# Prompt attention by chunks of 512 keys, and the setup loads in another order

## What is computed

```python
def diff_attend(q, k, v, q_pos, k_pos, lam):
    s = jnp.einsum('ntkgch,nskch->nkgcts', q, k, preferred_element_type=jnp.float32) * SCALE
    mask = k_pos[None, :] <= q_pos[:, None]
    s = jnp.where(mask, s, -jnp.inf)
    p = jax.nn.softmax(s, axis=-1)
    a = p[:, :, :, 0] - lam * p[:, :, :, 1]
    return jnp.einsum('nkgts,nskv->ntkgv', a, v.astype(jnp.float32))
```

## Time and profile before

| | us |
|---|---|
| median of 3 runs | 2490.93 |
| lowest, highest | 2490.03, 2493.18 |
| profiled execution | 2487.62 |
| its span, first to last instruction | 2485.8 |

### The profile page before, as it was taken

The page is one execution under the profiler, slowest core; times in us unless marked ns, Lnnn a source line. Parts: engine busy times, 40 slices in busy tenths (PEclk is TensorE's granted clock), DMA queues, the critical chain, the costliest instruction groups (busy, mean ns, idle before and its releaser), DMA issues. The chain is left out here.

```text
span 2485.8 us, 37618 instructions
## 1 busy us (share of the span) xinstructions
PE 2170.9 (87%) x13193; PEld 1995.5 (80%) x13193; DVE 1155.8 (46%) x1914; ACT 971.2 (39%) x1572; POOL 1279.6 (51%) x682
## 2 busy tenths in 40 slices
PE   4999999999279998999889987877777787898998
PEld 4999999999279998999889985655665666666998
DVE  3698889889845003222100005555555554346101
ACT  4455555555444112111121125555555554234111
POOL 2799999999733324433311125555455552224232
PEclk7999999999669999999989987888888887997999
DMA  6112111121223222223222230000000005882221
GB/s 234 51 54 65 60 60 60 48 63 53 84 60 122 69 94 88 69 77 94 90 82 95 86 128 26 18 26 18 17 26 17 9 1 155 255 262 76 60 77 70
DMA packets 182037, 192.51 MB, mean 77 GB/s; under 512 B 11435, under 2 KB 147060, under 8 KB 181332
## 3 DMA queue, kind: packets, MB, share of 16 engines
q1 hardware_dynamic: 181952, 191.48, 24.4%
HBM read 145.52 MB, written 47.63 MB: 78 GB/s over the span
## 5 line engine op out<-in xcount | busy, mean ns | idle before, releaser
L222 POOL TENSOR_TENSOR w_lo<-w_raw,w_hi 128x1024 fp32r<-128x1024 f32 x116 | 279.6, 2411 | 603.3 <-ACT w_hi L218 603.3
L242 PE MATMUL ps<-Hhi,w_hi 128*128 128x352 f32 x1704 | 560.5, 329 | 18.3 <-POOL w_lo L222 11.7
L242 PE MATMUL ps<-Hhi,w_lo 128*128 128x352 f32 x1704 | 550.9, 323 | 0.0
L242 PE MATMUL ps<-Hlo,w_hi 128*128 128x352 f32 x1704 | 549.9, 323 | 0.0
L777 DVE SCALAR_TENSOR_TENSOR ps<-U,dww,ps 128x512 f32<-128x512 f32 x608 | 403.1, 748 | 0.0
L218 ACT ACTIVATE w_hi<-w_raw 128x1024 fp32r<-128x1024 f32 x116 | 122.1, 1053 | 665.7 <-PE ps L242 244.6
L696 POOL TENSOR_TENSOR pool_acc<-pool_acc,prod 128x1024 f32<-128x1024 f32 x144 | 346.3, 2405 | 31.0 <-ACT prod L645 22.7
L242 PEld LDWEIGHTS ps<-Hhi,w_hi 128*128 128x128 f32 x1704 | 321.9, 189 | 27.9 <-POOL w_lo L222 18.4
L242 PEld LDWEIGHTS ps<-Hlo,w_hi 128*128 128x128 f32 x1704 | 323.1, 190 | 2.1
L242 PEld LDWEIGHTS ps<-Hhi,w_lo 128*128 128x128 f32 x1704 | 322.1, 189 | 0.0
L645 ACT ACTIVATE prod<-U,dww 128x1024 f32<-128x1024 f32 x176 | 197.0, 1147 | 249.8 <-POOL pool_acc L696 143.3
(11 more groups left out here) (237 smaller groups left out, 3876.4 us busy)
## 6 DMA issues: line engine op xcount, KB each, us to landing
w_raw<-conv_w_in SPq DMA_DIRECT2D x48, 512.0 KB, 4.1
w_raw<-attn_w_in SPq DMA_DIRECT2D x40, 512.0 KB, 4.7
kpage<-cache_k SPq DMA_DIRECT2D x64, 256.0 KB, 3.0
vpage<-cache_v SPq DMA_DIRECT2D x64, 256.0 KB
res<-Y SPq DMA_DIRECT2D x2, 4224.0 KB, 21.4
gate<-sg SPq DMA_DIRECT2D x16, 528.0 KB, 4.0
sgl<-gate SPq DMA_DIRECT2D x16, 528.0 KB, 3.7
xres<-res SPq DMA_DIRECT2D x16, 528.0 KB, 3.9
```

The costliest lines, as they stand in the source:

```text
L222: pool.tensor_tensor(wlo[s][:, :, :], raw[s][:, :, :], whi[s][:, :, :].bitcast(F32), ALU.subtract).then_inc(w_lo, 1)
L242: mm = pe.matmul(ps[:, 3 * dst + c, 0:CH], w[:, k, :], r(k)[:, c * CH:(c + 1) * CH], start=start and k == 0 and w is whi[s] and r is rhs_h ...
```

## The change

Attention is written in steps y = 0 .. 47 per group, twelve per head. A tile of up to 512 keys is one step as before; a wider one is two: its first 512 keys, then the rest with the mask. Every step uses one pair of banks, alternating. The second step of a wide tile takes the minimum of the two negated maxima (L1720), and the sums and weights of its first step are corrected by e = exp(new negated maximum - old negated maximum): a distance on DVE (L1723), an exponential on ACT (`weight`, L1647), two operations on DVE for the sums (L1732, L1734), and on POOL two scalings of the first 512 keys, of p1 by T0 x e / sum (`N_U`, L1740 on DVE) and of p0 by e. `stats` has 20 columns per tile and 32 tiles. The squares of the sums are taken once per head. `LAG` is 5 steps. `p0` has eight buffers of the widths needed, `p1` four. `coefficients` stands after `maxes` on DVE. The query's parts for the next head are made at step 1 instead of tile 4, new values at step 9, before `hi`.

In the setup, weights are loaded after the small loads, `stg` and the write of Y after the square roots; x tiles share semaphores in groups; the roots, reciprocals and the spread come before the turning of `dwin`; `stg` lies in another place and is turned in the convolution block, after PE's first unit; its copies stand behind the norm on ACT and DVE, and the wait for the written Y is on ACT and DVE there.

The diff, cut to its core:

```diff
-                for s, kind in ((0, 0), (1, 1)):
-                    sp.dma_start(raw[s][:, :, :], conv_src(0, kind)).then_inc(raw_in[s], 16)
                 for r, name, n in ((C_NG1, "norm_g", 16), ...
...
+                sp.dma_start(dwin[:, :], a["conv_dw_w"][0]).then_inc(dw_in, 16)
                 sp.dma_start(ptab[:, :], a["page_table"].rearrange("(o b) p -> o (b p)", o=1)).then_inc(lam_in, 16)
-                sp.dma_start(stg[:, :, :], st_src).then_inc(st_loaded, 16)
+                for s, kind in ((0, 0), (1, 1)):
+                    sp.dma_start(raw[s][:, :, :], conv_src(0, kind)).then_inc(raw_in[s], 16)
                 sp.wait_ge(xe_act, NXT)
                 sp.wait_ge(xe_dve, NXT)
+                sp.wait_ge(Norm.std_ready, 1)
+                sp.dma_start(stg[:, :, :], st_src).then_inc(st_loaded, 16)
                 sp.dma_start(res_d[0], Y[:, :, :]).then_inc(res_out[0], 16)
-                sp.wait_ge(res_out[0], 16)
...
                         unit_by_tile(pe, n, e, e, norms[0])
+                        if first and s == 0:
+                            turn_state()
                         pe.wait_ge(sg_done, j)
...
+                act.wait_ge(st_dve, JT // 4)
+                act.wait_ge(res_out[0], 16)
...
-        LAG = 2
+        LAG = 5
+        UNITS = 12
+        VALUES = {10: (0, (0,)), 11: (0, (1, 2)), 12: (0, (3,)),
+                  17: (1, (0, 1)), 18: (1, (2, 3)), 19: (1, (4, 5)), 20: (1, (6, 7))}
+        OUTPUTS, TOTALS, SUMS = {13: 0, 21: 1}, {14: 0, 22: 1}, {15: 0, 23: 1}
+        NEW_VALUES, NEXT_Q = 9, 1
...
+        def score_ap(x, n, c):
+            return ps[:, 2 * (unit_of(x, n) % 2) + c, 0:width(x, n)]
...
+                    if u >= 2:
+                        pe.wait_ge(exp_done, 2 * NU * g + 2 * (u - 2) + 2)
...
+                def exp(g, x, n, c):
+                    if n == 0:
+                        act.wait_ge(mx_done, 2 * NU * g + 2 * unit_of(x, n) + c + 1)
+                    else:
+                        act.wait_ge(run_done, 4 * GH * g + wides(x) + 1)
+                    if n == 0 and c == 0 and x >= QT:
+                        act.wait_ge(tg_done, NU * g + tgroups(x - QT)[-1][0] + 1)
+                    if n == 0 and c == 1 and x >= 4:
+                        act.wait_ge(comb_done, NX * g + x - 3)
...
+                def weight(g, x):
+                    act.wait_ge(dist_done, 4 * GH * g + wides(x) + 1)
+                    act.activation(stat(x, N_E, 2), stat(x, N_D, 2), ACT.Exp).then_inc(weight_done, 1)
...
+                        for c in range(2):
+                            exp(g, x, n, c)
+                        if n == 1:
+                            weight(g, x)
...
+                    if 0 <= y - LAG < top:
+                        hi(g, y - LAG)
...
+                    if n == 1:
+                        dve.wait_ge(mx_done, 2 * NU * g + 2 * u + 2)
+                        dve.tensor_tensor(stat(x, N_NM + 2, 2), stat(x, N_NM, 2), stat(x, N_NM + 2, 2), ALU.min
+                                          ).then_inc(run_done, 1)
+                        dve.wait_ge(run_done, 4 * GH * g + wides(x) + 1)
+                        dve.tensor_tensor(stat(x, N_D, 2), stat(x, N_NM + 2, 2), stat(x, N_NM, 2), ALU.subtract
+                                          ).then_inc(dist_done, 1)
...
+                    if wide:
+                        dve.wait_ge(weight_done, 4 * GH * g + wides(x) + 1)
+                        step_up(dve.tensor_tensor(stat(x, N_ES, 2), stat(x, N_E, 2), stat(x, N_SA, 2), ALU.mult))
+                        step_done()
+                        step_up(dve.tensor_tensor(stat(x, N_S, 2), stat(x, N_ES, 2), stat(x, N_SB, 2), ALU.add))
+                        step_done()
...
+                    if y < top:
+                        maxes(g, *tile_of(y))
+                    if 0 <= y - 1 < top and is_last(y - 1):
+                        coefficients(g, tile_of(y - 1)[0])
+                    if 0 <= y - LAG < top:
+                        lo(g, y - LAG)
...
+                    if last:
+                        pool.tensor_scalar(b[:, 0:512], b[:, 0:512], stat(x, N_U), stat(x, N_R1),
                                            ALU.mult, ALU.mult).then_inc(pn_done, 1)
+                        pool.tensor_scalar(a[:, 0:512], a[:, 0:512], stat(x, N_E), 1.0,
+                                           ALU.mult, ALU.mult).then_inc(pn_done, 1)
+                    pool.tensor_scalar(b[:, last:w], b[:, last:w], stat(x, N_T0), stat(x, N_R1),
+                                       ALU.mult, ALU.mult).then_inc(pn_done, 1)
```

More of the change, by code:

```diff
@@ L615, in _, with turn_state, tiles @@
                 sp.wait_ge(keep_out, 16)
+                sp.wait_ge(res_out[0], 16)
             @block.tensor
             def _(pe):
[L619 removed]
+                def turn_state():
+                    pe.wait_ge(st_loaded, 16)
+                    for m in range(JT // 2):
+                        if m >= 2:
+                            pe.wait_ge(st_act if m % 2 == 0 else st_dve, m // 2)
+                        for s in range(2):
+                            for h in range(2):
+                                c0 = (2 * s + h) * SR
+                                mm = pe.transpose(ps[:, 6 + m % 2, c0:c0 + SR],
+                                                  stg[:, h, (2 * m + s) * P:(2 * m + s + 1) * P], ident[0:SR, 0:SR])
+                        mm.then_inc(st_turned, 1)
+                def tiles(i, first=False):
                     for s in range(2):
@@ L629, in _ @@
                         unit(pe, n + 2, e, e, h_hi, h_lo)
+                tiles(0, first=True)
+                with pe.Fori(1, JT // 2) as i:
+                    tiles(i)
                 pe.wait_ge(sg_done, JT)
@@ L639, in _ @@
                 norm_act(act, norms[0])
+                for m in range(0, JT // 2, 2):
+                    act.wait_ge(st_turned, m + 1)
+                    act.activation(state[:, 2 * m:2 * m + 2, :].rearrange("p j n -> p (j n)"), ps[:, 6, 0:4 * SR], ACT.Copy
+                                   ).then_inc(st_act, 1)
+                act.wait_ge(st_dve, JT // 4)
+                act.wait_ge(res_out[0], 16)
                 def products(i, s, part):
@@ L737, in _ @@
                     dve.wait_ge(*norms[0].lo(k))
+                for m in range(1, JT // 2, 2):
+                    dve.wait_ge(st_turned, m + 1)
+                    dve.tensor_copy(state[:, 2 * m:2 * m + 2, :].rearrange("p j n -> p (j n)"), ps[:, 7, 0:4 * SR]
+                                    ).then_inc(st_dve, 1)
+                dve.wait_ge(res_out[0], 16)
                 for s in range(2):
@@ new lines, in scores @@
+                    dst = [score_ap(x, n, c) for c in range(2)]
+                    masked = n == parts(x) - 1
+                    for m, (ql, kr) in enumerate(((qhi, khi), (qhi, klo), (qlo, khi))):
+                        for c in range(2):
+                            rows_ = slice(HD * c, HD * c + HD)
+                            mm = pe.matmul(dst[c], ql[s][rows_, i * P:(i + 1) * P], kr[rows_, 512 * n:512 * n + w],
+                                           start=m == 0, stop=m == 2 and not masked)
+                            if m == 2 and not masked:
+                                mm.then_inc(s_done, 1)
@@ L1694, in _ @@
+                dve_step.leave(NG - 1)
+                for y in range(PRE, NU + TAIL):
+                    step(NG - 1, y, NU)
             @block.gpsimd
@@ L1714, in step @@
+                def step(g, y, top):
+                    j = y // UNITS
+                    if y < top and is_last(y):
+                        join(g, tile_of(y)[0])
+                    if y % UNITS == NEXT_Q and UNITS * (j + 1) < top:
                         q_lo(pool, g, j + 1)
-                    if x % NX == NEW_VALUES and x < top:
-                        v_lo(g + x // NX)
-                for x in range(PRE):
-                    step(0, x, NX)
+                    if y % NU == NEW_VALUES and y < top:
+                        v_lo(g + y // NU)
```

351 lines of the change are left out of this document (165 added, 186 removed).

## The result

| | before | after |
|---|---|---|
| median, us | 2492.05 (4 runs) | 2612.56 (4 runs, 2610.8 to 2612.8) |
| span of the profiled execution | 2485.8 | 2610.2 |
| mean granted clock of PE | 0.912 | 0.881 |

The change makes the kernel slower, by a ratio of 1.0482 (95% interval 1.0464 to 1.0501). The prediction said 2555 us, range 2505 to 2590. The direction is right, the size is not: 64 us more were forecast, 120.5 came.

What follows compares the result with a forecast made beforehand. Bound by setup and, in attention, a ring of ACT and DVE waiting for each other. 2487.6 + 74 attention - 5 group changes + 2 start and tail - 7 setup = 2551.6 profiled, so median 2555 us, range 2505 to 2590.

Steps and rivals of the forecast that it cites:

- The ring is not cut: Attention: ACT and DVE still wait for each other in turn, 12 rounds per head instead of 8.
- M, E and H: Attention links per head: maximum to exponential +3.2 us, exponentials to high part +1.7, high part to low part's end +1.9.
- 36.4 us for a head without blocking: Attention: the ring's sum per head after the change, from 34.9 before, without DVE's waits for POOL.
- 8 x 0.2 for the coefficients: Attention before: an estimated 0.2 us per tile before the next maximum, eight tiles per head, summed as 1.7 us.
- Small operations behind POOL: Attention: DVE's two-input operations wait for POOL's running instruction to finish, adding 3.5 us per head.
- rival 1: Attention: POOL's scalings do not block DVE; 38.0 us per head, 2526 us in total; chance 0.15.
- PE late: -4.9: Attention: DVE's 4.9 us per head of waiting for PE vanishes, as PE has a chunk in hand.
- The +0.9 for the output copy: Attention on ACT: query copy and one output copy, 2.0 us, get about 1.1 of cover; +0.9 us per head.
- Changes of group: -5: Attention: the three changes of group pay about 5 us instead of some 6.4; -5 us in all.
- Setup: -7: Setup: norm begins near 37.8 us instead of 50.60, the state's turning holds PE about 5.5; net -7 us.
- Rival 3: Attention: PE stays at its lower clock and the ring waits for it; some 44 us per head, 2620; chance 0.07.

Runs made afterwards that it cites:

- e5: The changed kernel with ACT's high part of chunk y-5 moved before the exponentials of y; ratio 1.0015 to the kernel before.
- e4: The changed kernel with POOL's scalings and additions of the weights cut to 128 columns, part of them left out; ratio 1.0297 to the kernel before.
- e3: The changed kernel with PE's totals one step later and ahead of its turn; ratio 1.0346 to the kernel before.
- e9: The changed kernel with v_lo before the join on POOL and totals one step later on PE; 2540.2 us, ratio 1.0219 to the kernel before.
- e2: The changed kernel with POOL's v_lo moved ahead of the join of the same step; ratio 1.0366 to the kernel before.
- e1: The kernel before with the setup part of the change alone, attention as before; 2478.9 us, ratio 0.9966.
- e6: The changed kernel with v_lo before the join, totals one step later, and ACT's high part before the exponentials; 2424.6 us, ratio 0.9732 to the kernel before.
- e7: As e6, with DVE's minimum, distance and first coefficient written as one-column TENSOR_SCALAR operations; ratio 0.9758 to the kernel before.

## Why the prediction was right and wrong, step by step

- **The ring is not cut; M, E and H.** Right. The plain chunk has the predicted links within 0.02 us, and e5 shows that this ring is worth 116 us here. The predicted 36.4 us for a head without blocking fits: e4 has 39.4 with the totals' wait still in, and e3 puts that wait at 3.0. The difference is an estimate, since no run has both. (One slip: 8 x 0.2 for the coefficients is 1.6, not 1.7.)
- **Small operations behind POOL, 3.5 us per head.** The mechanism is right, the size a little high: tile 6's minimum was to lose 1.65 and lost 1.5, tile 7's 0.35 and 0.65, tile 5's 0.5 and nothing: it starts within 0.05 us of a scaling's start and passes. The distances, which were to make the weight late by 0.7 and 0.8, last 0.23 us at most. The two minima make 2.2 us per head by these rows; e4 has 2.4.
- **Do POOL's one-input scalings block?** Yes, so rival 1 falls. POOL, then DVE, in the changed kernel:

```profile
1746.48 0.69 POOL L1792 TENSOR_SCALAR p<-p,stats 128x512 f32<-128x512 f32 x1
...
1746.82 0.36 DVE L1736 TENSOR_TENSOR stats<-stats,misc 128x1 f32<-128x1 f32 x1
```

  They end at 1747.17 and 1747.18, one of 32 such pairs with a scaling in this trace. So the trace agrees with the sentence of the Trainium skill (SBUF — State Buffer, "Who interferes with whom") on any GpSimd instruction that reads SBUF, for one input as for two. A scaling of 512 columns lasts 0.77 us, and such a hit no longer.
- **PE late: -4.9.** This step failed first. "PE has a chunk in hand" was argued from the scores alone, by what they depend on. Of PE's queue it left out `total`, which stands one step behind the output and holds the scores behind it. Before, it stood as close, but PE came to it when the squares were made (1.2 us of waiting in all); with a chunk in hand PE comes to it before they are made, and waits there: 3.5 us per head late by the rows, 3.0 by e3, instead of none. The lateness did not vanish, it came under another name. (The low clock behind the wait is part of it.) The +0.9 for the output copy was the same place seen from ACT only. e3 puts it at 34 us in all. Even with both stalls mended (e9) DVE still waits 36.9 us for PE, 2.3 per head.
- **Changes of group: -5.** This step failed second, and in sign. The price of a change was taken over from before, about 5 us each. The new place of `v_lo`, step 9 behind a join that depends on DVE's next step and one chunk ahead of its use, was in the diff and was not followed through POOL's queue to PE. Measured: 10.0 to 12.6 us for the values alone in the three changes of group, and 3.8 more for the keys in the head before; e2, which mends half of the values' wait, takes 29 off. With the totals mended and this wait halved (e9) the kernel is at 2546.6, 8 us under the forecast.
- **Setup: -7.** The norm's start was right to 0.3 us. The turning of the state holds PE from 57.70 to 62.68 us, 5.0 of the 5.5 taken, and PE's second unit starts at 62.68 instead of 70.25: 7.6 us won, as forecast. 11 us arrive at attention in the changed kernel and 9.6 in e1; where the other 2.0 to 3.4 come from was not traced, and attention starts anywhere between 1466.6 (e4) and 1475.3 (e3) in the kernels with this setup.
- **Rival 3, the clock falls to give 2620.** The number came close and the reason is another. The clock did fall (0.84 to 0.73), but the ring did not come to wait for PE's slower products: e3 takes out 34 us at a clock of 0.70, e9 66 at 0.73. The low clock goes with PE standing still at its stalls and in the ring, and is 0.84 again in e6. But it is not without price: just after a stall the scores are slow (0.80 instead of 0.50 us for a pair), and in e6 a wait of 4.6 us is followed by 15 us at half clock with PE busy nearly throughout. This part lies inside the 34 and 29 us of e3 and e2, and no run separates it.

The account of the 120.5 us: 63 forecast (2555 against the 2492 of these runs), 66 in the two missed waits as far as e9 removes them, and -8 by which the forecast was too heavy against e9. Since e9 keeps half of the values' wait, the forecast's other terms were too heavy by more than 8.

## What to carry to other kernels

Where engines with queues in order wait for each other, a deeper lag between stages does not open the ring as long as each queue puts the new work first; here it was enough to put the older work first in one of them, ACT's. Look at the order of a step before its depth. For each instruction that an edit moves, and for each that an engine now reaches earlier, name who waits for it and what stands behind that waiter: both misses here were short operations (eight products of one column, one subtraction of 2.3 us) that held PE's next scores. And when a wait is said to vanish, ask of every other instruction in that engine's queue whether it now waits in its stead.

## What the runs showed of the hardware

- A DVE operation with two SBUF inputs, on one or two numbers per partition, lasts until POOL's running instruction ends: 1.67 us instead of 0.16, behind additions and behind scalings with one input (78 of 94 cases in the changed kernel). The 16 that start 0.02 to 0.05 us after a scaling are not held. TENSOR_SCALAR forms on one column were not blocked (0.20 to 0.22 us in e7), nor was RECIPROCAL (0.15 to 0.16 us in 33 cases beside POOL), nor the low part, which reads PSUM and SBUF (0.69 us at 1771.08, beside POOL's scalings).
- The granted clock of a stretch ran from 0.70 to 0.84 with PE busy 433 and 490 of 550 us (e3, e6), and did not follow the time: 2575 us at 0.70, 2613 at 0.73.
- After PE had idled 4.6 us in e6, its granted clock went from 0.99 to 0.50 and stayed there for some 15 us of nearly full work; a pair of score products of 512 keys took 0.79 to 0.80 us in such stretches and 0.50 outside them.
